# A block-triangular inverse on smaller tiles of the PE array: 32x32 in place of 64x64

## The reference, cut to what matters

```python
def step(s, inp):                       # s: (heads, value, key), one token at a time
    r_t, w_t, k_t, v_t, kk_t, b_t = inp
    sa = jnp.einsum('bhvk,bhk->bhv', s, kk_t)
    s = (s * w_t[:, :, None, :] - sa[..., None] * b_t[:, :, None, :]
         + v_t[..., None] * k_t[:, :, None, :])
    y = jnp.einsum('bhvk,bhk->bhv', s, r_t)
    return s, y
```

## Time and profile before

| | us |
|---|---|
| median of 3 runs | 2996.67 (2994.12 to 2999.45) |
| the profiled execution | 2989.08 |
| its span, first to last instruction | 2987.3 |
| scan stage, first x1 to the end of the last block | 455.0 to 978.0 |

### The profile page before, as it was taken

One profiled execution on the slowest core, in us unless ns is written; L12 is line 12 of the kernel. 1 busy time (PEld: TensorE's weight loads), 2 busy tenths in 40 slices (PEclk: granted clock), 3 DMA queues, 4 the chain that ended last, 5 costly groups with the idle time before them and its releaser, 6 DMA issues. The chain is left out here.

```text
span 2987.3 us, 65358 instructions
## 1 busy us (share of the span) xinstructions
PE 2668.4 (89%) x27700; PEld 2333.9 (78%) x27700; DVE 1118.9 (37%) x3300; ACT 613.8 (21%) x1622; POOL 501.3 (17%) x706
## 2 busy tenths in 40 slices
PE   6999988888888698599999999999999999999991
PEld 2555557777777344599999999999999999999991
DVE  1389526767676233413212321321221232132125
ACT  4010035555555233000100000010010000001002
POOL 0684004435444100000000000000000000000002
PEclk9999978999999898699999999999999999999995
DMA  6432210000000410687758668766876866777553
GB/s 217 168 99 84 85 46 4 4 4 5 3 5 21 164 55 28 233 308 270 257 205 313 239 237 293 262 236 228 284 255 224 313 238 235 263 270 257 203 209 134
DMA packets 227316, 519.69 MB, mean 174 GB/s; under 512 B 9629, under 2 KB 34205, under 8 KB 226778
## 3 DMA queue, kind: packets, MB, share of 16 engines
q1 hardware_dynamic: 218170, 483.47, 44.0%
q0 software_dynamic: 6384, 21.83, 2.9%
q10 hardware_dynamic: 2480, 10.06, 0.9%
HBM read 489.00 MB, written 26.33 MB: 173 GB/s over the span
## 5 line engine op out<-in xcount | busy, mean ns | idle before, releaser
L1934 PE MATMUL ps_h<-xT,w1c 128*128 128x144 f32 x4096 | 568.4, 294 | 60.2 <-issue 58.9
L1934 PEld LDWEIGHTS ps_h<-xT,w1c 128*128 128x128 f32 x4096 | 537.8, 196 | 63.9 <-issue 61.8
L1934 PE MATMUL ps_h<-xT,w3c 128*128 128x144 f32 x4096 | 551.6, 289 | 0.0
L1934 PEld LDWEIGHTS ps_h<-xT,w3c 128*128 128x128 f32 x4096 | 528.8, 193 | 0.0
L1944 PE MATMUL ps_ye<-he,w2c 128*128 128x144 f32 x4096 | 513.9, 286 | 0.0
L1944 PEld LDWEIGHTS ps_ye<-he,w2c 128*128 128x128 f32 x4096 | 505.8, 190 | 0.4
L1888 DVE TENSOR_TENSOR u<-ps_h,sig 128x144 f32<-128x144 f32 x256 | 78.8, 308 | 981.9 <-ACT sig L1771 981.8
L1771 ACT ACTIVATE sig<-ps_h 128x144 f32<-128x144 f32 x256 | 74.5, 291 | 1146.2 <-PE ps_h L1934 1146.2
L557 PE MATMUL front_bank<-wide,win 128*128 128x384 f32 x912 | 298.1, 489 | 2.0 <-DVE wide L441 2.0
L557 PEld LDWEIGHTS front_bank<-wide,win 128*128 128x128 f32 x912 | 173.4, 191 | 127.8 <-issue 9.6
L1802 POOL DMA_INDIRECT acc<-ys,idx_s x16 | 25.7, 1609 | 1129.9 <-ACT ye_p L1759 1062.2
(11 more groups left out here) (264 smaller groups left out, 3169.9 us busy)
## 6 DMA issues: line engine op xcount, KB each, us to landing
w1c<-in_w SPq DMA_DIRECT2D x64, 2048.0 KB, 8.1
w3c<-in_w SPq DMA_DIRECT2D x64, 2048.0 KB, 13.7
w2c<-in_w SPq DMA_DIRECT2D x64, 2048.0 KB, 13.8
ada<-in_ada_w SPq DMA_DIRECT2D x24, 1024.0 KB, 6.4
prow<-probsT ACTq DMA_DIRECT2D x17, 576.0 KB, 8.0
win<-in_w_in SPq DMA_DIRECT2D x19, 512.0 KB, 4.2
z<-in_x_all SPq DMA_DIRECT2D x3, 1536.0 KB, 14.8
acc<-zero SPq DMA_DIRECT2D x9, 512.0 KB, 7.9
```

Source lines behind the costliest of these rows:

```text
L1934: ins = eng.matmul(ps_h[g % 2][:, off:off + SLOTS], w[:, b, k, f * P:(f + 1) * P], xT[:, k], start=(k == 0), stop=(k == KT - 1))
```

## The change

Level 1 to 4 merge blocks that never leave a 32x32 block on the diagonal, so both products of these levels need only the four 32x32 diagonal squares of the two chunks. Before, each 64x64 square was multiplied whole. Now each of these squares is a product by itself (index q, partitions 32q to 32q+31), on a tile of the array of its own. Level 5 needs one off-diagonal square of each 64x64 block, the upper one in one direction and the lower one in the other; now only that is computed. What the rest of the bank holds is copied along, and the mask keeps it out of the inverse.

```diff
@@ -706,6 +706,9 @@
     post_done = sem("post_done")
 
     H = (slice(0, HS), slice(HS, P))
+    HB = HS // 2
+    Q = [slice(q * HB, (q + 1) * HB) for q in range(4)]
+    Q_COL = [slice((q % 2) * HB, (q % 2 + 1) * HB) for q in range(4)]
     NB = CT * NB_T
     N_SQ, N_SUM, N_MAX, N_ROOT, N_INV, N_TURN, N_COPY = 1, 5, 6, 7, 8, 9, 10
     FIRST, LAST = -2, NB + 8
@@ -1131,8 +1134,13 @@
                 else:
                     eng.wait_ge(trans, 8 * b + 2 * (lv - 2) + g + 1)
                 for h in range(2):
-                    for c in range(2):
-                        ins = mm(ps_g[H[c], g, h * HS:(h + 1) * HS], ab[H[c], b3, g, h, 2], t0[H[c], b2, g, h])
+                    for q in range(4):
+                        if lv < LEVELS - 1:
+                            lo = h * HS + Q_COL[q].start
+                            ins = mm(ps_g[Q[q], g, lo:lo + HB], ab[Q[q], b3, g, h, 2, Q_COL[q]], t0[Q[q], b2, g, h, Q_COL[q]])
+                        elif q % 2 == g:
+                            lo = h * HS + Q_COL[q].start
+                            ins = mm(ps_g[Q[q ^ 1], g, lo:lo + HB], ab[Q[q], b3, g, h, 2, Q_COL[q ^ 1]], t0[Q[q], b2, g, h, Q_COL[q]])
                 ins.then_inc(x_ps, 1)
 
         def level_t(b, lv):
@@ -1140,12 +1148,12 @@
             for g in range(2):
                 eng.wait_ge(x_sb, 10 * b + 2 * (lv - 1) + g + 1)
                 for h in range(2):
-                    for c in range(2):
-                        out = ps_g[H[c], g, (2 + h) * HS:(3 + h) * HS]
+                    for q in range(4):
+                        lo = (2 + h) * HS + Q_COL[q].start
                         if lv < LEVELS - 1:
-                            ins = mm(out, t1[H[c], b2, g, h], xw[H[c], g, h])
-                        else:
-                            ins = mm(out, xw[H[c], g, h], t1[H[c], b2, g, h])
+                            ins = mm(ps_g[Q[q], g, lo:lo + HB], t1[Q[q], b2, g, h, Q_COL[q]], xw[Q[q], g, h, Q_COL[q]])
+                        elif q % 2 != g:
+                            ins = mm(ps_g[Q[q ^ 1], g, lo:lo + HB], xw[Q[q], g, h, Q_COL[q ^ 1]], t1[Q[q], b2, g, h, Q_COL[q]])
                 ins.then_inc(t_ps, 1)
 
         def solve(b):
```

## The result

The kernel after takes 3041.9 us (median of 4 runs, 3037.4 to 3043.7), the kernel before 2996.7 us in the same rounds: a ratio of 1.0148, 95% interval 1.0131 to 1.0166. It is 45 us slower where 8 us faster was forecast. The profiled execution has a span of 3041.4 us against 2987.3; that one of before was a quick one, 7.6 us under its median, so the profiles differ by 54 us.

A forecast was written before the change was run, and what follows sets the result against it. Neither TensorE nor VectorE alone bounds a block, but each of five levels is a chain of waits. 12.3 us less in the scan, +4 for the clock, gave -8: 2988.5 us, range 2967 to 3024.

The forecast's parts named there:

- That needs TensorE to start a record every 8 ns.: Levels 1 to 4: 32 records a stage on four tiles, 8 steps each, take 0.26 us at this rate.
- pace: Rival: small-tile records start no quicker than 15 ns, stages stay as long, switches are extra: +30 us, 3026; chance 0.16.
- The sum: Scan's level-by-level gains: 0.23 us a short block, 0.50 a long one, 12.3 us less; clock +4, so -8 us.
- a floor of about 25 ns from start to start: Rival on TensorE's record starts, from the Trainium skill: loss about 100 us, 3095 us; chance 0.02.
- The switches: Changes between 32 and 64 tiles on TensorE, 14 new per short block: 0.095 us each beyond the columns.
- The price of a step: One tile's step on TensorE: 58 ns at 64 columns, 108 at 128, so 33 ns estimated at 32.
- Level 5: step B's first half is 0.2 us sooner, and so ztmp and zst: -0.17: Last level of each block: x5 takes 0.14 us, VectorE's work and the copy come sooner, 0.17 us less.
- Level 1 (-0.07): First level of each block: t1's halves done 0.1 and 0.2 us sooner, x2 0.07 us sooner.
- level 3 of the short block (+0.01): Third level of short blocks: t3 0.02 us later, products start 0.06 later and end 0.01 later.
- Levels 2 and 3 of the long block: Blocks where post_mid stands between levels 2 and 3: -0.18 us in level 2, -0.07 in level 3.
- The clock term: Scan: TensorE streams half as long in changed stages; 20 us more at half clock allowed, +4 us.
- hidden: Rival: gains in levels 1, 3 and 5 held by ScalarE or VectorE; only 2.7 us come, 2996; chance 0.16.

The follow-up runs named there:

- pad64: The kernel before with 64 added four-column 64x64 products a block in levels 1 to 4, 960 instructions a block: 3139.3 us, ratio 1.0469.
- lv5: The kernel after with small tiles in level 5 alone, levels 1 to 4 on 64x64 products as before: 2989.4 us, ratio 0.9974.
- mix: The kernel after with small tiles only in level 5, plus levels 2 and 3 in the 21 blocks that call post_mid: 2911.5 us, ratio 0.972.
- lv125: The kernel after with small tiles in levels 1, 2 and 5, levels 3 and 4 on 64x64 products: 3019.8 us, ratio 1.0079.
- lv1235: The kernel after with small tiles in all levels but the fourth, which is on 64x64 products: 3034.6 us, ratio 1.014.
- after_shift: The kernel after with 32 unread 32x32 products (128 TensorE instructions) added behind the scan: 2958.3 us, ratio 0.9882.
- after_fill: The kernel after with two unneeded products in TensorE's idle time between t2 and x3 of the 15 blocks without post_mid: 2950.4 us.
- before_shift: The kernel before with 32 unread 32x32 products (128 TensorE instructions) added behind the scan: 2905.3 us, ratio 0.9707.
- before_fill: The kernel before with two unneeded products in TensorE's idle time between t2 and x3 of the 15 blocks without post_mid: 2908.5 us.
- lv5_shift: Small tiles in level 5 alone, with 32 unread 32x32 products (128 TensorE instructions) added behind the scan: 2898.5 us, ratio 0.9688.
- burst: The kernel before with 2048 unread 32x32 products (8192 instructions) in a row behind the scan: 3109.9 us, ratio 1.0374.
- lv125_fill: Small tiles in levels 1, 2 and 5, with two unneeded products between t2 and x3 of the 15 blocks without post_mid: 2918.0 us.

## Why the prediction was wrong, point by point

- The step that failed: **"That needs TensorE to start a record every 8 ns."** The records do, 6 or 7 ns apart within a group of four tiles, and x1 took 0.50 us where 0.65 would have said "pace". But I asked only how fast the array starts records, and not how fast the program reaches it. The sum charged nothing for 256 more instructions in a block. At 13.8 ns each they are 3.5 us, in blocks that had 3.0 us to spare (12.7 less 9.7). With the clock at full on both sides a short block lost 1.7 us (14.30 against 12.61). Over 21 blocks that is 36 us, an estimate, of the 37.2 us by which the scan grew.
- The rows of before could have told it. 100 packets over the scan's 523 us were in reach, and "issue" waits of up to 4.5 us at 14 passes of the loop over the experts; I read neither.
- The rival "pace" had the sign and nearly the size (+30), for another reason: an even spacing of records. The records come in a rush and then not at all. The rule that stood beside it, a floor of about 25 ns from start to start (the Trainium skill, TensorE: Matmul & The Clock Gate, Part 1), does not hold over several tiles: x1's 32 records start within 0.31 us, 10 ns apart. On one tile the trace does not go against it: from a record to the fourth after it, which is the step of a tile, the median is 32 ns.
- The switches were right: x1's last record starts at 555.99 + 0.50 - 0.19 = 556.30 and solve's first load at 556.42, 0.12 us later as forecast; solve's last record at 557.15 and t1 at 557.30, 0.15. A change between 32 and 64 costs what one between 64 and 128 does.
- The price of a step, "64 columns cost 50 ns and the rest about 8", was right in size by luck. The line went through 64 and 128 moving columns on the same 64x64 tile, 58 and 108 ns, and below 64 it does not go on: four moving columns there cost as much as 64 (pad64). The step of a 32x32 tile did fall, to 32 ns, but there the weights were halved together with the columns.
- "Level 5: step B's first half is 0.2 us sooner, and so ztmp and zst: -0.17" was wrong in its second half. VectorE in level 5 of a short block, lv5:

```profile
516.66 1.14 DVE L1044 TENSOR_TENSOR_SCAN cum<-cst,dsig 128x256 f32<-128x256 f32 x1
517.73 0.26 DVE L1014 TENSOR_TENSOR ztmp<-ps_rr,zst 128x128 f32<-128x128 f32 x1
```

  ztmp starts the moment cum ends, 0.92 us after x5 (516.81) and 0.99 before the change, where cum likewise ends last. Step B is sooner and is not waited for. So -0.07, which lv5's short blocks show.
- Level 1 (-0.07) and level 3 of the short block (+0.01) are too small to be seen behind the stops. Levels 2 and 3 of the long block were right (0.2 us in mix). What the change really has to give is some 0.1 us in a short block and 0.3 in a long one, 7 us or so, a little over half of the 12.3 us in the sum, and the supply takes five times that.
- The clock term had the right sign and was under-sized as an amount of time: half clock in the scan rose from 28 to 85 us, I allowed 20 more. The price was too low as well: a drop of 3.4 us cost 1.5 us in lv125 (14.16 against 12.65), 0.44 us for each us where I had 0.21. What it cost in the kernel after is mostly hidden by the stops, but lv1235 lost 42 us with half the added "issue" waits on ps_g (16 us, against 33 in the kernel after). So it is likely, and not shown, that without the stops the drops would have taken much of the same time.
- What stays open: the 15.7 us that the profile after loses behind the last x1. 10.3 of them are in the last block and the closing work, and TensorE was at half clock for 244 us behind that x1 against 207 before. From the last x1 to the loop over the experts after_shift and after_fill are 11 and 12 us longer than before_shift and before_fill too; but lv5, which gains, is 10.8 us longer behind its last x1 in its profile, and lv5_shift 1 us up to that loop. The cause is open.
- A slip in a rival: "hidden" comes to 2998 by its own terms (2.7 us less, 4 us more), not to 2996. It changes no chance.

## What to carry to other kernels

Count instructions as well as columns: splitting a product into smaller tiles multiplies them, and on this engine 256 of them took 3.5 us and more to arrive. Divide a stage's instructions by its time before the change: at 704 in 12.7 us (18 ns each) there was room for a fifth more (840 still took 12.6 us with the clock held up), not for a third (968 took 14.3). A wait that ends with "issue" in the middle of a row of equal products, or at the top of a loop, is the program arriving late, and where a loop lies in the program can be worth more than what stands in it.

## What the hardware showed that I had not expected

- TensorE's program comes in pieces of 256 instructions, 3.48 to 4.03 us apart in the burst, where it must be waited for: 13.8 ns an instruction over 8192.
- A loop can wait for its own code, up to 4.5 us at 14 of its passes, and moving it by 128 instructions took 90 us off the kernel.
- A product of four columns with 64x64 weights takes a tile as long as one of 64 columns: 61 ns a step.
- VectorE's nbt and nbh take 1.35 or 1.92 us, by whether GpSimd's kd starts 0.02 us or more ahead of them.
- Products put into TensorE's idle 1.3 us kept its clock at full in the blocks that had them (all 12 compared in lv125_fill, against 6 of them in lv125), at no cost in time where there was room: the scan of before_fill is as long as before's (511.8 and 512.6 us).
